# Two transformer blocks on one core: the second block's mixer steps in another order, its output product in three parts, and the overflow test moved

## What is computed

```python
def second_block(x, positions, ...):
    for l in range(DEPTH_2):                                   # 2 layers
        mix = hybrid_mixer(x, tabs, w_in[l], ..., w_o[l])
        x = layer_norm(DEEPNORM_ALPHA * x + mix, ln1_g[l], ln1_b[l])
        moe = hier_moe(x, rg_w, rg_b, re_w, re_b, w_gate, w_up, w_down)
        x = layer_norm(DEEPNORM_ALPHA * x + moe, ln2_g[l], ln2_b[l])

def hybrid_mixer(x, ...):
    u = x @ w_in                                               # one product, cut in ten parts
    o_a = mla_mixer(a_cq, a_ckv, a_kpe, ...)                   # 8 heads, causal
    o_b = dsa_mixer(b_q, b_k, b_v, b_qi, b_ki, b_wi, ...)      # 4 heads, on the 64 best keys
    o_c = dilated_mixer(c_qkv, ...)                            # 4 heads, three windows each
    return concatenate([o_a, o_b, o_c]) @ w_o
```

## Time and profile before

| | us |
|---|---|
| median of 3 runs (1836.46 to 1839.66) | 1838.58 |
| the profiled execution's own time | 1839.03 |
| its span in the profile | 1837.2 |
| PE busy | 1562.6 (85%) |
| DVE busy | 497.8 (27%) |
| ACT busy | 332.6 (18%) |

### The profile page before, as it was taken

One profiled execution on the slowest core, in us unless ns is written; L12 is line 12 of the kernel. 1 busy time (PEld: TensorE's weight loads), 2 busy tenths in 40 slices (PEclk: granted clock), 3 DMA queues, 4 the chain that ended last, 5 costly groups with the idle time before them and its releaser, 6 DMA issues.

```text
span 1837.2 us, 18685 instructions
## 1 busy us (share of the span) xinstructions
PE 1562.6 (85%) x7706; PEld 867.0 (47%) x7706; DVE 497.8 (27%) x1076; ACT 332.6 (18%) x697; POOL 0.2 (0%) x4
## 2 busy tenths in 40 slices
PE   6999999675666656598998899999898978999997
PEld 3557768331222211175677543443665666444434
DVE  5112432200111100035552322121254623221123
ACT  1413110100000000022221322111131322121112
POOL 0000000000000000000000000000000000000000
PEclk9999999877887878799998899999998989999998
DMA  9314518799999999942230699999222213999980
GB/s 390 133 46 188 225 54 349 305 427 429 428 427 428 427 428 428 427 197 92 92 138 1 255 415 387 396 382 384 76 99 92 92 46 141 392 395 402 378 350 24
DMA packets 35307, 494.42 MB, mean 269 GB/s; under 512 B 3920, under 2 KB 4176, under 8 KB 4688
## 3 DMA queue, kind: packets, MB, share of 16 engines
q1 hardware_dynamic: 34640, 491.08, 65.3%
q10 hardware_dynamic: 576, 2.05, 0.3%
HBM read 492.06 MB, written 1.05 MB: 268 GB/s over the span
## 4 chain that ended last, share of the span: by engine, by line
PE 70%; DMA 21%; DVE 6%; ACT 2%; issue 1%; DVEq 0%; ACTq 0%
PE PS L528 23%; DMA A<-ring_d 20%; PE PS L1312 12%; PE PS L1335 6%; PE PS L831 3%; PE PS L533 3%; PE PS L1188 3%; PE PS L1297 3%; PE PS L1350 3%; PE PS L1177 2%; PE PS L979 2%; PE PS L1014 1%; PE PS L594 1%; PE PS L1141 1%; PE PS L540 1%
## 5 line engine op out<-in xcount | busy, mean ns | idle before, releaser
L528 PE MATMUL PS<-A 128*128 128x256 f32 (+7 forms) x1840 | 477.8, 419 | 5.4 <-DVE A L2124 1.9
L528 PEld LDWEIGHTS PS<-A 128*128 128x128 f32 (+2 forms) x1840 | 340.9, 199 | 130.1 <-issue 80.5
L831 PE MATMUL PS<-A 128*32 128x512 f32 x1536 | 243.0, 770 | 152.1 <-DMA A<-ring_d 152.1
L1312 PE MATMUL PS<-A 128*64 128x512 f32 x1024 | 226.8, 595 | 0.1
L831 PEld LDWEIGHTS PS<-A 128*32 128x32 f32 x1536 | 53.2, 126 | 329.6 <-issue 255.2
L1312 PEld LDWEIGHTS PS<-A 128*64 128x64 f32 x1024 | 71.6, 137 | 133.7 <-issue 132.1
L1335 PE MATMUL PS<-A 128*64 128x512 f32 x512 | 116.9, 599 | 0.0
L533 PE MATMUL PS<-A 128*128 128x128 f32 (+1 forms) x462 | 77.1, 302 | 43.6 <-DVE A L2026 8.5
L533 PEld LDWEIGHTS PS<-A 128*128 128x128 f32 (+1 forms) x462 | 58.8, 155 | 90.0 <-issue 44.3
L1790 DVE TENSOR_TENSOR A<-A,PS 128x512 f32<-128x512 f32 x8 | 5.5, 690 | 341.2 <-PE PS L831 341.2
L2190 DVE TENSOR_TENSOR A<-A,PS 128x256 f32<-128x256 f32 x32 | 13.5, 423 | 225.1 <-ACT A L2702 225.1
(11 more groups left out here) (328 smaller groups left out, 1242.9 us busy)
## 6 DMA issues: line engine op xcount, KB each, us to landing
A<-ring_d SPq DMA_DIRECT2D x228, 2048.0 KB, 12.3
A<-ring_d SPq DMA_DIRECT2D x2, 1312.0 KB, 18.7
A<-ring_d SPq DMA_DIRECT2D x2, 1280.0 KB, 16.3
A<-xT_d SPq DMA_DIRECT2D x2, 1024.0 KB, 8.9
A<-pf_d SPq DMA_DIRECT2D x4, 512.0 KB, 19.5
A<-p_d SPq DMA_DIRECT2D x1, 1278.5 KB, 5.6
A<-p_d ACTq DMA_DIRECT2D x1, 1232.0 KB, 12.1
A<-cT_d SPq DMA_DIRECT2D x1, 1024.0 KB, 20.1
```

Source lines behind the costliest of these rows:

```text
L528: ins = g.matmul(out, l, r, start=n == 0, stop=n == len(pairs) - 1)
L831: ins = g.matmul(ps[32 * e:32 * e + 32, :], rows_of(kk, e), wv[:, kk % 2, e, :], start=kk == 0, stop=kk == 7)
L1312: ins = g.matmul(ps[64 * s:64 * s + 64, :], XS2[u % 2][:, kk, c:c + 64], wv[:, kk % 4, s, :], start=kk == 0, stop=kk == 7)
```

## The change

There are four edits, and one that concerns only the code for overflow.

1. `AMONG` gives for each turn two lists, `front` and `behind`, which stand ahead of and behind `nr`/`tr`. Where a rotation stood behind its own projection, another projection or a transpose now stands between; the rounds `tk` are spread differently, and `dm` moves from turn 4 to turn 5.
2. The output product is in three parts: `wa` (mla rows, 4 of 8 row blocks, 8 products) in turns 8 and 9, a new `ws` (sel rows, 4 products) in turn 10, and `wb` as before.
3. `group_sum(15)` of each layer stands behind the overflow test instead of ahead of it, on PE, DVE and ACT.
4. At the first block's end, the load of the root's table and the squares, gains and column sums of quarters 0 and 1 stand ahead of the last half of `w_down`; and `p2` is loaded by SP, ahead of the fourth block of the second block's weights (`u`), instead of by ACT.

The overflow code uses other banks and another stretch of memory (`XD`), since `group_sum(15)`'s inputs must survive it; in these runs it is jumped over.

```diff
-        more = among[t] if t < len(among) else []
-        out += more[:len(more) // 2]
+        front, behind = among[t]
+        out += front
         if 0 < t <= len(units):
             out += [("nr", *units[t - 1]), ("tr", *units[t - 1])]
-        out += more[len(more) // 2:]
+        out += behind
...
-AMONG = [dilated(0) + TOPK[0:3], queries(2) + dilated(1) + TOPK[3:6], queries(3) + dilated(2) + TOPK[6:9], [("vc", 0, 0)] + TOPK[9:12],
-         [("vc", 0, 1)] + TOPK[12:16] + [("dm",)], dilated(3), dilated(4), dilated(5), [], [], [("wa", 0), ("wa", 1)], [("wa", 2), ("wa", 3)]]
+AMONG = [([("qa", 2), ("km", 2), ("da", 0)], [("qb", 2), ("db", 0)] + TOPK[0:2]),
+         ([("qa", 3), ("km", 3), ("da", 1)], [("qb", 3), ("db", 1)] + TOPK[2:4]),
+         ([("da", 2)], [("db", 2)] + TOPK[4:7]),
...
+         ([("da", 3)], [("db", 3)] + TOPK[13:16] + [("dm",)]),
...
+         ([("wa", 0), ("wa", 1)], []),
+         ([("wa", 2), ("wa", 3)], []),
+         ([("ws", b) for b in range(4)], []),
+         ([], [])]
...
-                for strand, u in (("mla", 3), ("sel", 1)):
-                    g.wait_ge(*at("ov", l, strand, u))
-                output(b, 0, 6)
+                g.wait_ge(*at("ov", l, "mla", 3))
+                output(b, 0, 4)
+
+            def ws(b):
+                g.wait_ge(*at("ov", l, "sel", 1))
+                output(b, 4, 6)
...
-                experts_pe(g, l, weights, arrived, finished, group, turn, full)
+                last_sum = experts_pe(g, l, weights, arrived, finished, group, turn, full)
                 overflow_pe(g, l, group, turn)
+                last_sum()
...
-            for p in range(16 + 3):
+            for p in range(16 + 2):
...
+            def last_sum():
+                sig.stage = f"e{l}"
+                group_sum(15)
...
+                        fresh("fsum")
+                        banks.hold("fsum")
+                        squares(0)
+                        squares(1)
             combine(3, 2)
             combine(3, 3)
-            for b in range(4):
+            for b in (2, 3):
                 ins = squares(b)
...
                     if x == 3 and half == 0:
-                        s.dma_start(V(ARENA2, P2N), p2_d).then_inc(*land("in8", "p2"))
...
+                        settle()
+                        s.activation(STAT[:, 62:63], EPS5, ACT.Sqrt, bias=0.0, scale=1.0).then_inc(*out())
+                        final_squares(0)
+                        final_squares(1)
+            final_squares(2)
+            final_squares(3)
...
+                if key == ("u", 0):
+                    q.wait_ge(*at("full", "gu", 3, 1, 1))
+                    q.dma_start(V(ARENA2, P2N), p2_d).then_inc(*land("in8", "p2"))
```

More of the change, by code:

```diff
@@ L433, in program @@
         XS2 = [take(8, 256) for _ in range(2)]
-        YEo = mem.top
         YE2 = [take(1024) for _ in range(2)]
+        PXo = mem.top
         PX2 = [take(8, 64) for _ in range(2)]
@@ L917, in tensor @@
                         combine(3, 1)
-            fresh("fsum")
-            banks.hold("fsum")
+                        fresh("fsum")
+                        banks.hold("fsum")
+                        squares(0)
+                        squares(1)
             combine(3, 2)
             combine(3, 3)
-            for b in range(4):
+            for b in (2, 3):
                 ins = squares(b)
@@ L1222, in turned_rows @@
                 return ins
-            steps = dict(wa=wa, kx=kx, cq=cq, ckv=ckv, cqsum=cqsum, kvsum=kvsum, kpe=kpe, vm=vm, qa=qa, km=km, qb=qb, ca=ca, cb=cb, kir=kir,
+            steps = dict(wa=wa, ws=ws, kx=kx, cq=cq, ckv=ckv, cqsum=cqsum, kvsum=kvsum, kpe=kpe, vm=vm, qa=qa, km=km, qb=qb, ca=ca, cb=cb, kir=kir,
                          vc=vc, bkr=bkr, ix=ix, da=da, db=db, sc=sc, sm=sm, tr=tr, pv=pv)
@@ L1412, in overflow_pe @@
                     for m in range(8):
-                        if m >= 4:
-                            g.wait_ge(*at("xrm", l, e, m - 4))
-                        group(PS[:, m % 4, 0:256], [(wd[:, f, m * 128:(m + 1) * 128], XHD[:, f, :]) for f in range(2)]) \
+                        if m >= 3:
+                            g.wait_ge(*at("xrm", l, e, m - 3))
+                        group(PS[:, (0, 1, 7)[m % 3], 0:256], [(wd[:, f, m * 128:(m + 1) * 128], XHD[:, f, :]) for f in range(2)]) \
                             .then_inc(*up("pe", "full", "xd", l, e, m))
@@ L1820, in vector @@
                 mixers_dve(v, l, out, settle, full, scale_rows, affine, square)
-                experts_dve(v, l, out, settle, full)
+                last_sum = experts_dve(v, l, out, settle, full)
                 overflow_dve(v, l, settle)
+                last_sum()
                 sig.stage = f"n{l}"
@@ L2249, in experts_dve, with last_sum @@
             note("dve", "e_end", l, "dve")
+            def last_sum():
+                sig.stage = f"e{l}"
+                group_sum(15)
+            return last_sum
         def overflow_dve(v, l, settle):
@@ L2453, in scalar, with final_squares @@
             settle()
+            def final_squares(b):
+                rows = slice(2 * b, 2 * b + 2)
+                s.wait_ge(*at("ex", 3, b))
+                s.activation(T[:, rows, :], X[:, rows, :], ACT.Square, bias=0.0, scale=1.0).then_inc(*out("fsq", b))
+                if b < 2:
+                    settle()
+                    for k in (2 * b, 2 * b + 1):
+                        ins = s.activation(X[:, k, :], X[:, k, :], ACT.Copy, bias=0.0, scale=p1("g_fin")[:, k:k + 1])
+                    ins.then_inc(*out("fg", b))
             def sines(i):
@@ L2510, in scalar @@
                 mixers_act(s, l, out, settle, full, square, root, affine)
-                experts_act(s, l, out, full)
+                last_sum = experts_act(s, l, out, full)
                 overflow_act(s, l)
+                last_sum()
                 sig.stage = f"n{l}"
```

11 lines of the change are left out of this document (7 added, 4 removed).

## The result

The changed kernel takes 1768.62 us (median of 4 runs, 1768.05 to 1769.90) against 1837.62 for the kernel before (4 runs, 1836.46 to 1839.66): a ratio of 0.9624, 95% interval 0.9608 to 0.9641. Forecast were 1777 and 1769 to 1798.

What follows compares the result with a forecast made beforehand. DMA bounds the first block's experts, PE's work the second's; in the mixers PE sets the pace but waits. From 1839.0, 37.1 + 21.2 - 1.8 + 3.0 + 2.1 + 0 = 61.6 gave 1777; range 1769 to 1798.

Steps and rivals of the forecast that it cites:

- Waits in the mixers: In both layers' mixers, three rotations' waits on ACT and two transposes' waits on DVE go: 37.1 us.
- the new wait: At turn 6 of each mixer, PE waits for DVE's division for dil 1: 0.9 us, twice, -1.8.
- Clock in the mixers: In both mixers, the slow granted clock behind the waits goes with them: 21.2 us.
- The rule weighed there: Short idle spells between product groups can make the mixers' clock swing; then 21.2 us stay lost and the sum is 40.4.
- First block's end: Behind the first block's experts, the moved p2 load saves 3.0 us and the moved squares 2.1.
- the load: With p2 moved to SP, the first block's last w_down lands 3.0 us earlier.
- the squares: At the first block's end, square 2 on ACT begins 2.1 us earlier.
- The overflow test: At each layer's end, testing ahead of the last sum changes nothing: 0 us, bounds +0.6 and -2.6.
- By the rule the stall comes in either order: At the overflow test, the branch stalls wherever it stands; the sum would be 1.2 us less.
- the test hides: Rival: the overflow test begins under the last down-projection, saving 2 x 2.6 us, so 1772; chance 0.1.

Runs made afterwards that it cites:

- The halves: Two runs on the kernel before: the new turns 0 to 5 alone, 1807.15 us; the new turns 8 to 11 alone, 1811.22 us.
- the kernel with this part alone: The kernel before with p2 loaded by SP behind the last w_down, and squares 0 and 1 with their gains moved up: 1829.94 us.
- the test alone: The kernel before with only the overflow test put ahead of the last sum: 1831.93 us, ratio 0.9965.
- the version without pair 14 moved: The changed kernel with two search rounds moved to turns 3 and 4 and a share of group 2 put behind the last sum: 1764.60 us.

## Why the prediction missed its range

- **Waits in the mixers**: right, 35.9 gone net of the new wait (17.4 + 18.5) where 35.3 were forecast. That all three rotations and both transposes were covered, and that turn 6 would cost 0.9, came out.
- **Clock in the mixers**: right, 22.5 (10.5 + 12.0) for 21.2. The halves show it belongs to the waits. The rule weighed there, from the Trainium skill ("TensorE: Matmul & The Clock Gate", section "A second HAM failure mode: psum-queue depth-cycling"), is not borne out in this kernel: 665 products in small groups, with 2.8 us of gaps in 129, stood at 1.00.
- **First block's end**: right in kind, 5.9 (7.7 in the kernel with this part alone) for 5.1. Over all kernels the load gave 3.2 for 3.0, and the squares 3.1 for 2.1: the term left out the column sums that moved with them.
- **The overflow test**: this step failed. "I take 0 for each layer, bounds +0.6 and -2.6" measured -3.3 and -3.3, outside its own bounds. Two things were missed. I had seen that PE could begin the test while the products ahead still run, and gave that only 0.10 as a rival. Yet in the earlier trace rows the issue stood where PE had nothing queued, and the diff put 16 products of 3.58 us ahead of it. The trace of before shows the overlap already: its branch began at 1293.88, while the sum's products ran until 1294.47. And the bound left out the clock: each mixer wait was priced with the slow spell behind it, PE's stop of 3.2 us behind the sum (2.6 of it issue) was not, and its spell was worth 1.3. With both in the sum, 2 x (2.1 + 1.3) more, the forecast would have been 1770.
- The Trainium skill's rule ("Runtime: NRT & Kernel Launch", section "Instruction fetch mechanics") that a taken branch stalls until its target has been fetched, where that isn't in the fetched window, agrees with PE's records of 3.4 to 5.8 us and the fetch of 16 KB under each. "By the rule the stall comes in either order", which I drew from it, is true of the sequencer and false of the products: they ran on beneath it.
- No rival decided the result; "the test hides" had the right mechanism, with the price lacking the clock.

## What to carry to other kernels

Put a branch right behind the longest run of products that is ready, not behind a short one with a copy still to come; what it then still costs is what of it is left at the end of that run, here 0 to 1.35 us. Other stops of a sequencer were not tried. When a stop of PE is priced, price it with the slow clock that follows in the rows: here the test with its 2.6 us of issue cost 3.6 to 3.9, and 37 us of waits cost 60 (the 58 gained and the 1.8 of the new wait). And look for list orders in which a projection stands right ahead of the step that reads its copy: here one other step of PE between them (a projection, a rotation or a transpose) was enough, as the engine that copies wasn't held by something else.

## What the runs showed of the hardware that was not expected

- PE's taken branch over the overflow code has a record of 3.35 to 5.81 us, between builds and between layers of one build; those of DVE and ACT take 0.04 to 0.07. DVE's next work is late all the same. In the changed kernel its branch was done at 1259.6, and its next copy came 3.0 us behind that, with no releaser named, though the sum that it copies was complete at 1261.2:

```profile
1262.55 0.69 DVE L2222 COPY A<-PS 128x512 f32<-128x512 f32 x1 [2.97 <-issue]
```

In the changed kernel's layer 1 it is 2.9 us, with the test alone 2.9 in both layers, and 2.8 in layer 0 of the version without pair 14 moved. What DVE waits for in that time isn't shown.

- PE's wait of 0.9 us at turn 6 was followed by no slow spell (clock 1.00 from 845 to 974 us), nor was its stop of 1.33 with the test alone: the four products behind it took 1.97, as behind the 0.50 of the changed kernel. The mixers' waits of 2.7 to 4.2 us were, and so was the stop of 3.2 us behind the last sum.
